# Splitting the moving operand of the output projection into 512 and 32 columns instead of 272 and 272

## What is computed

```python
def decoder_layer(x, pool_hist, conv_hist, start, attend, lp):
    h = rmsnorm(x, lp['g_mix_pre'])
    proj = h @ lp['w_in']                      # 2048 -> 4096: pooling input, q, k, v
    ...
    pooled = pool_mix(u, pool_hist, start, lp['w_pool'], lp['pool_scale'])
    attn = attend(q, k, v).transpose(0, 2, 1, 3).reshape(B, L, ATTN_DIM)
    mix = jnp.concatenate([pooled.astype(x.dtype), attn.astype(x.dtype)], axis=-1) @ lp['w_out']
    x = x + rmsnorm(mix, lp['g_mix_post'])
    f, new_conv = conv_ffn(rmsnorm(x, lp['g_ffn_pre']), conv_hist, lp['w_gate'], lp['w_up'],
                           lp['conv_w'], lp['conv_b'], lp['w_down'])
    x = x + rmsnorm(f, lp['g_ffn_post'])
```

## Time and profile before

| | us |
|---|---|
| median of 2 runs | 2847.12 |
| lowest and highest | 2845.56, 2848.68 |
| profiled execution, span | 2843.8 |
| PE busy in it | 2740.9 (96%) |
| PEld busy | 2416.9 (85%) |
| DVE busy | 1172.0 (41%) |
| ACT busy | 710.6 (25%) |
| the seven groups, 1344 matmuls | 168.4 |

### The profile page before, as it was taken

The page is one execution under the profiler, slowest core; times in us unless marked ns, Lnnn a source line. Parts: engine busy times, 40 slices in busy tenths (PEclk is TensorE's granted clock), DMA queues, the critical chain, the costliest instruction groups (busy, mean ns, idle before and its releaser), DMA issues.

```text
span 2843.8 us, 51136 instructions
## 1 busy us (share of the span) xinstructions
PE 2740.9 (96%) x19408; PEld 2416.9 (85%) x19408; DVE 1172.0 (41%) x1852; ACT 710.6 (25%) x1226; POOL 120.9 (4%) x265
## 2 busy tenths in 40 slices
PE   8999999979999999789999999999999999999994
PEld 8876767654444699789999999999999999999994
DVE  7433222340111433584343434444444343434357
ACT  5211111250111222342222222222222222222231
POOL 3000000000000000130000000000000000000002
PEclk9999999999999999899999999999999999999997
DMA  4455556407777442222222222222322223232321
GB/s 162 138 200 211 207 197 219 152 8 234 242 239 245 147 156 88 59 71 89 86 89 87 86 89 86 87 89 78 96 81 92 85 89 88 87 86 89 87 91 74
DMA packets 146616, 347.23 MB, mean 122 GB/s; under 512 B 16608, under 2 KB 16608, under 8 KB 146048
## 3 DMA queue, kind: packets, MB, share of 16 engines
q1 hardware_dynamic: 144480, 338.35, 37.2%
q0 software_dynamic: 2080, 8.14, 0.8%
HBM read 334.32 MB, written 12.10 MB: 122 GB/s over the span
## 4 chain that ended last, share of the span: by engine, by line
PE 93%; DVE 4%; DVEq 1%; ACT 1%; issue 0%; DMA 0%; POOL 0%; SPq 0%; ACTq 0%; POOLq 0%
PE ps_acc L705 28%; PE ps_acc L682 18%; PE ps_a L705 14%; PE ps_b L705 14%; PE ps_a L747 8%; PE ps_a L859 4%; PE ps_b L859 4%; PE ps_a L682 1%; PE ps_b L682 1%; PE ps_acc L801 1%; DVE act_lo L957 1%; DVE region L1362 0%; DVE w_lo L261 0%; DVE region L1247 0%; DVE region L1366 0%
## 5 line engine op out<-in xcount | busy, mean ns | idle before, releaser
L261 DVE TENSOR_TENSOR w_lo<-w_raw,w_hi 128x512 fp32r<-128x512 f32 x724 | 502.1, 705 | 1217.2 <-ACT w_hi L255 1214.2
L255 ACT ACTIVATE w_hi<-w_raw 128x512 fp32r<-128x512 f32 x724 | 445.5, 628 | 1397.7 <-PE ps_acc L682 475.9
L705 PE MATMUL ps_acc<-act_hi,w_hi 128*128 128x272 f32 x1472 | 308.4, 291 | 33.8 <-DVE act_lo L957 18.9
L705 PE MATMUL ps_acc<-act_lo,w_hi 128*128 128x272 f32 x1472 | 306.9, 290 | 0.0
L705 PE MATMUL ps_acc<-act_hi,w_lo 128*128 128x272 f32 x1472 | 304.8, 288 | 0.0
L682 PE MATMUL ps_acc<-act_hi,w_hi 128*128 128x272 f32 x1280 | 273.6, 295 | 2.0 <-DVE scratch L968 1.1
L682 PE MATMUL ps_acc<-act_hi,w_lo 128*128 128x272 f32 x1280 | 264.6, 288 | 0.0
L682 PE MATMUL ps_acc<-act_lo,w_hi 128*128 128x272 f32 x1280 | 263.9, 288 | 0.0
L705 PEld LDWEIGHTS ps_acc<-act_hi,w_hi 128*128 128x128 f32 x1472 | 232.5, 190 | 36.5 <-issue 22.1
L682 PEld LDWEIGHTS ps_acc<-act_hi,w_hi 128*128 128x128 f32 x1280 | 199.8, 188 | 49.7 <-issue 48.3
L747 PE MATMUL ps_a<-region,q_blk 128*32 128x256 f32 x1024 | 233.2, 382 | 2.3 <-ACT q_blk L423 2.3
(11 more groups left out here) (210 smaller groups left out, 3981.1 us busy)
## 6 DMA issues: line engine op xcount, KB each, us to landing
w_raw<-units SPq DMA_DIRECT2D x724, 256.0 KB, 2.6
region<-kcache SPq DMA_DIRECT2D x128, 512.0 KB, 4.2
region<-vcache SPq DMA_DIRECT2D x128, 512.0 KB, 4.5
region<-xT SPq DMA_DIRECT2D x8, 544.0 KB, 6.7
region<-xT SPq DMA_DIRECT2D x4, 1088.0 KB, 8.4
yT<-region SPq DMA_DIRECT2D x8, 544.0 KB, 2.7
ext_out<-region POOLq DMA_DIRECT2D x8, 339.5 KB, 4.5
kT_out<-scratch POOLq DMA_DIRECT2D x8, 272.0 KB, 5.8
```

The source lines that it names most:

```text
L255: act.activation(w_hi[:, s], w_raw[:, s], ACT.Copy).then_inc(hi_ready, 1)
L261: dve.tensor_tensor(w_lo[:, s], w_raw[:, s], w_hi[:, s].bitcast(F32), ALU.subtract).then_inc(lo_ready, 1)
L705: mm = pe.matmul(banks(mt, odd)[:, n, 0:HN], w[:, s, i, cols], half(a[:, kt], n), start=kt == 0 and w is w_hi and a is hi, stop=kt == 2 * ...
```

## The change

In the seven groups of the loop, n = 0 takes the 512 prompt columns and n = 1 the 32 decode columns. The first fills a whole bank, the second uses 32 columns of the next. VectorE's copy of a tile becomes two instructions, one for each bank, with `acc_free` counted behind the second. The order of the matmuls, their number, the weights' path and the first group stay.

```diff
@@ -280,6 +280,14 @@
         def two(ap):
             return ap.rearrange("p (a n) -> p a n", a=2)
 
+        def rows(ap, n):
+
+            return ap[:, SEQ:NT] if n else ap[:, 0:SEQ]
+
+        def row_bank(mt, n, odd=0):
+
+            return banks(mt, odd)[:, n, 0:NS if n else SEQ]
+
 
         @block.sync
         def _(sp):
@@ -662,7 +670,7 @@
 
         @block.tensor
         def _(pe):
-            def group(G, q, nu, hi, lo, ready=None, after=None, k0=0, first=False, odd=0, units=None, prev=1):
+            def group(G, q, nu, hi, lo, ready=None, after=None, k0=0, first=False, odd=0, units=None, prev=1, by_rows=False):
 
                 for u in units or range(nu):
                     k = K_OUT[u] if units else k0 + u
@@ -679,8 +687,9 @@
                             cols = slice(mt * P, (mt + 1) * P)
                             for w, a in ((w_hi, hi), (w_hi, lo), (w_lo, hi)):
                                 for n in range(2):
-                                    mm = pe.matmul(banks(mt, odd)[:, n, 0:HN], w[:, s, i, cols], half(a[:, kt], n),
-                                                   start=kt == 0 and w is w_hi and a is hi,
+                                    out = row_bank(mt, n, odd) if by_rows else banks(mt, odd)[:, n, 0:HN]
+                                    src = rows(a[:, kt], n) if by_rows else half(a[:, kt], n)
+                                    mm = pe.matmul(out, w[:, s, i, cols], src, start=kt == 0 and w is w_hi and a is hi,
                                                    stop=kt == 2 * nu - 1 and w is w_lo)
                         if u == nu - 1 and mt == 0:
                             mm.then_inc(acc_done, 1)
@@ -897,7 +906,7 @@
             pool_product(3)
             group(G_OUT, Q_POOL, 8, act_hi, act_lo, ready2, first=True, odd=1, units=range(4, 8))
             with pe.Fori(1, 8) as g:
-                group(g + G_OUT, 2 * g + Q_OUT, 8, act_hi, act_lo)
+                group(g + G_OUT, 2 * g + Q_OUT, 8, act_hi, act_lo, by_rows=True)
             sum_squares(2 * KT)
 
 
@@ -1217,10 +1226,15 @@
 
             dve.memset(sq_sum, 0.0)
 
-            def mix_tiles(g, q, k, odd=0):
+            def mix_tiles(g, q, k, odd=0, by_rows=False):
                 for mt in range(2):
                     tile_done(dve, g + G_OUT, mt, q, k)
-                    dve.tensor_copy(two(tile_of(acc, 2 * g + mt)), bank(mt, odd)).then_inc(acc_free, 1)
+                    t = tile_of(acc, 2 * g + mt)
+                    if by_rows:
+                        dve.tensor_copy(rows(t, 0), row_bank(mt, 0))
+                        dve.tensor_copy(rows(t, 1), row_bank(mt, 1)).then_inc(acc_free, 1)
+                    else:
+                        dve.tensor_copy(two(t), bank(mt, odd)).then_inc(acc_free, 1)
                     dve.drain().then_inc(mix_out, 1)
                 for mt in range(2):
                     dve.drain()
@@ -1231,7 +1245,7 @@
             with dve.Fori(1, 8) as g:
                 for u in range(8):
                     split_lo(dve, 2 * g + Q_OUT, u + LEAD)
-                mix_tiles(g, 2 * g + Q_OUT, 7)
+                mix_tiles(g, 2 * g + Q_OUT, 7, by_rows=True)
             mean_square(2)
             root_mean(2)
```

## The result

The changed kernel takes 2911.24 us (2 runs, 2909.88 to 2912.61) against 2847.12 us: ratio 1.0221, 95% interval 1.0201 to 1.024, so it is slower by 64 us.

The account below looks back on a forecast made before the run. TensorE's matmul stream bounds the kernel: 672 pairs at 340 instead of 250.6 ns add 60.1 us, the last copy 0.1; +60.2 us on the 2847.12 us median gives 2907.3 us, range from 2886 to 3 us above 2915.

Parts of the forecast that it names:

- The frame: Seven-group stage is TensorE matmuls alone, so extra time is paid fully: 168.4 to 228.5 us, everything after keeping its length.
- The load slot: In each seven-group pair, the 32-column matmul lasts as long as the next 512's weight load, 112 ns; one load ahead.
- the prediction's lower bound: Cheapest pair of the forecast's own case in the seven groups: 213.3 + 3 + 107 = 323 ns, giving +48.7 us.
- The 512 columns: The 512-column fp32r matmul of each seven-group pair takes 228 ns, chosen nearer 225 than 236.
- The upper bound: For the 512-column matmul in the seven groups: 236 ns, if the loss above bare columns grows with the columns.
- the prediction's own hint: From modelled durations of 272-column matmuls: their 12 ns loss is 9 ns slower streaming and 3 ns between matmuls.
- The copies: VectorE's two copies per tile add 0.12 us; thirteen of fourteen lie under matmuls, the last adds 0.1 us to the chain.
- The hidden second load: Rival: both loads of a seven-group pair hide under the 512 columns; pair 244 to 261 ns, 2843 to 2854 us; chance 0.07.
- The cheaper slot: Rival: seven-group fp32r load partly hidden or half as long; pair 284 to 323 ns, 2870 to 2896 us; chance 0.13.
- the dearer pair: Rival in the seven groups: two records with two loads (452 ns, +135 us) or half clock (640 ns, +262 us); chance 0.07.
- What would show it: Expected timeline signs in the stage: 512 starts 228 ns before its 32, next 512 112 ns later; 1344 matmuls in 228 us.

Follow-up runs that it names:

- e7: Kernel before with every fp32r pair split 288 + 256 and PSUM reads of both halves in two instructions: 2840.6 us against 2847.95 us, ratio 0.9974.
- e1: The sweep: changed kernel with its group loop written out and seven splits, from 272 + 272 to 512 + 32; the seven groups took 189.44 us.
- e2: Changed kernel (512 + 32) loading only 32 of 128 weight columns in the seven groups: 2855.11 us beside 2847.16 us for the kernel before; pair 263.3 ns.
- e3: Kernel before's 272 + 272 split, loading only 32 of 128 weight columns in the seven groups: 2845.64 us beside 2847.16; stage 167.26 us for 168.38.
- e4: Kernel before with only VectorE's copy of each tile made two instructions of 272 columns: 2848.72 us beside 2847.16; stage 168.38 us as before.
- e6: Changed kernel, loop written out, loading 128, 96, 64, 32, 64, 96 and 128 weight columns in the seven groups, which took 206.9 us.

## Why the prediction was right

The forecast was 2907.3 us, the result 2911.24.

**The frame** held: the stage is PE alone, its time is paid in full, and what follows is as long as before. What it said of 2%, that this is about what a measurement of this kernel can tell from no change, is not so: e7 stands clear of the kernel before by 0.26%, with 8 and 17 runs.

**The load slot** was the argument, and its mechanism is shown: one load is ahead, not two; the load of 128 columns fills a slot of its own when fewer columns stream beneath it than take as long (192 and less in e1, where 240 take 112 ns already). Forecast 112 ns, measured 108.9. The 112 were read from fp32 rows of L870 and L878; fp32r's own two loads had shown 0.11 us, and were the nearer row. The 107 ns in the prediction's lower bound stand in no row; the shortest mean slot of a full load in these runs is 108.2.

**The 512 columns** were the term that was mis-sized: 228 ns forecast, 235.6 measured. Between the bounds 225 (one loss a matmul) and 236 (a loss that grows with the columns) I chose near the lower, because I put the loss down to the load that lies beneath. e2 and e3 show that it isn't: with a quarter of the load, 512 columns still take 235.2 ns and 272 take 124.4. The upper bound was right almost to the nanosecond, and the sweep shows why: from 256 to 512 columns the time goes from 117.6 to 235.5 ns, in proportion, with no fixed part to be seen. Even the prediction's own hint, 9 ns of slower streaming and 3 ns between matmuls, gives 213.3 + 17 + 3 = 233 ns when the 9 grow with the columns. That part of the two errors cancels is luck. The pair comes to 344.4 ns, not 340: -3.1 and +7.6 ns. Over 672 pairs that is 3.0 us, and it is the difference between +60.1 forecast and +63.0 measured in the stage. The rest of the 3.9 us between forecast and result is no larger than the shift ahead of the stage, 1.4 us in this profile and 3.3 in e4's.

**The copies** were costed at 0.1 us on the chain. From the start of the first to the end of the second it is 0.79 us where one took 0.72, and e4 shows the stage unchanged to 0.01 us with split copies. In the changed kernel PE has no wait in the stage either.

**The hidden second load**, the rival on the other side, is out: every one of the 672 slots has its load in it. The rule of the Trainium skill (TensorE: Matmul & The Clock Gate, section Back-to-back issue gap), N / 2.4 + 2.5 ns with a floor of 25 ns and no load in it, fails with it: its estimate for the pair is 241 ns, against 344.4 measured. **The cheaper slot** is out by the 108.9 ns measured, and e6 has 0.84 ns for each weight column. Of **the dearer pair**, the clock stayed at 1.00 with 544 columns in 344 ns, and there is one record for each matmul, 19408 in all.

**What would show it** had one mistake. I wanted the 32's record 228 ns behind the 512's, and the next 512's 112 ns behind that. The records stand 316.8 and 27.6 ns apart, since the 512's starts while its weights are still coming. The starts of the loads give the two terms, those of the matmuls only their sum.

What is left open is why an fp32r column costs 0.46 ns at the full clock, where one a cycle is 0.417. e2 and e3 take the size of the load away as its cause, though a load of 32 columns still lay under each matmul. The work of VectorE and ScalarE beside it is out too: in the trace of before, each of the 24 matmuls of a unit has its own distance to the next, the same within 1 ns in all 56 units, whether VectorE works meanwhile (419 matmuls) or not (770), and ScalarE likewise (282 and 938). That the loss belongs to fp32r isn't shown. The columns without it, fp32 at the full clock and fp32r at half clock, both go at 0.83 ns each, so a limit of one column in 0.46 ns for any type would not show in them. No run here tells the two apart.

## What to carry to other kernels

A matmul of few moving columns costs the load of the next weights, not its columns: here 109 ns for 128 weight columns, at 192 fp32r columns and at 32 alike. So where a length needs two matmuls, split it into parts that each cover a load, and don't fill the first to the bank's limit and leave a small rest. To read such a price from a trace, take the starts of the loads and find a stretch of small matmuls for the slot. What lies above the bare columns may be fixed or grow with them; one length can't tell, and here it grew.

## What the runs showed that I had not expected

At 2.4 GHz, fp32r columns go at 0.46 ns each, from 256 columns (117.6 ns) to 512 (235.5 ns), 10% above one a cycle, with 128 weight columns loaded beneath and with 32 (with 96 and 64, 512 columns took 232 to 233 ns); at 1.2 GHz the same 272 columns take 226.7 ns, with nothing above. The loss isn't noise. By the load starts, the 512-column matmuls of the changed kernel take 231 to 240 ns by a fixed pattern: each of the three products has its own value, it alternates with the input tile, and it repeats in all seven groups (for the third product 231 and 233 ns, for the second 238 and 240). The 272-column ones of the kernel before have a fixed pattern too, 121 to 129 ns, that repeats with each unit of 24. With the places of the operands changed, as in 288 + 256, the mean moves by 1%. Which property of the place matters isn't settled, nor whether it is the place.
